# Summing the log forget gates of all blocks and heads with two matrix products, later in the index stage

## The chip, the cores and the metric

The kernel runs on one core of one Trainium2 chip. The metric is the device time of one execution in microseconds (us); the figure of a kernel is the median of its runs.

## The reference: what is computed

A trunk of two identical layers works on 1024 tokens behind 16 learned meta tokens. Each layer has one input projection, four groups of attention heads A, B, C and D, an output projection and a layer norm. The change touches one ingredient of group A (forgetting attention) alone: the running sum of the log forget gates, which is added to the logits as a decay.

```python
logf = jax.nn.log_sigmoid(h['a_f'].astype(jnp.float32) + b_f.astype(jnp.float32))
decay = jnp.transpose(jnp.cumsum(logf, axis=1), (0, 2, 1))
out_a = causal_dense_attention(qa, ka, va, key_valid, HEAD_DIM ** -0.5, decay)
# in it, for each block of 128 queries:
logits = logits + cq[..., None] - decay[:, :, None, :]
```

The part of a query, `cq`, is the same for all its keys and falls out of the softmax, so the kernel adds only the part of the keys. Group C picks 256 keys for every query by a score, a sum over 8 index heads of relu(q k) times a weight; the stage that computes this score is called the index stage here, and it is where the running sum is made.

## The kernel before, in words

Tokens stand in 9 blocks: block 0 has the 16 meta tokens, blocks 1 to 8 have 128 each. A class `Plan` writes one list of items by hand, and each engine walks through this list in order, doing its own part of every item and waiting on semaphores for the others. So the order of the list is the order of work on every engine; nothing reorders it.

The index stage (`Plan.index`) runs over four pairs of index heads, p = 0 to 3, and in each over the query blocks i = 8 down to 2. An item `ix` is: TensorE multiplies the block's queries with the keys in chunks of up to 512 columns into PSUM banks 0 to 3 (L993), two chunks in flight (`next_slot` alternates between banks 0, 1 and banks 2, 3); ScalarE applies the relu into one of three rows in SBUF (L1181); VectorE multiplies with the head's weight and accumulates the score (L1372, L1375). Between them stand fill items, taken from the list `fills[p]`, one after each `ix` while they last: a projection tile of a weight ring (L967) or a block of values of group A (`token_block`, L934). They use bank 4 (`P_BANK`), and ScalarE empties it. For p = 0 there are five fills, after i = 8 to 4, so that none stands after i = 3 or i = 2; for p = 1 and 2 it is the same.

The item `cum` stands after `ix` of p = 0, i = 3. VectorE computes log sigmoid of 9 blocks x 8 heads = 72 values for each of 128 token positions (L1340 to L1356, each instruction linked to the one ahead by a semaphore), with one exponential on ScalarE in between (L1135). TensorE then forms the running sums: for each group of three blocks, `c`, one bank of 8 rows (heads) x 384 columns (tokens), and for each block `b` up to it a product of the block's 128 x 8 gates with ones or with the upper triangle (L957), 18 products in all. ScalarE copies banks 0, 1 and 2 out with three instructions (L1138 to L1140). SyncE stores the 8 x 1040 result to DRAM (`falls`, L815) and, once it is stored, loads it back spread over 128 partitions (`load_fall`, L746), two rows for each pair of heads of group A. GpSimd adds the causal triangle to it (L1521), and the softmax of group A reads it (VectorE, L1449).

The semaphores around it: TensorE waits for `cum_in` (VectorE's last gate instruction) and for the banks to be free; ScalarE waits for `fe_in` ahead of the exponential and for `cum_full` ahead of the copies; the next `ix` on TensorE waits for `cum_free`, the last of these copies; SyncE's store waits for `cum_free` too.

Of the kernel before, what the change touches and what calls it, by code (L numbers as in the profile page):

```python
# [7 lines left out]
ALU = mybir.AluOpType  # L8
ACT = mybir.ActivationFunctionType

D_MODEL, SEQ, DEPTH = 1024, 1024, 2
N_META, BLK = 16, 128
NB = SEQ // BLK + 1
NTOK = SEQ + N_META
KT = D_MODEL // BLK
HD, NH = 64, 8
# [19 lines left out]
P_BANK = 4  # L36
# [15 lines left out]
def tok0(b):  # L52
    return 0 if b == 0 else N_META + BLK * (b - 1)


def rows_of(b):
    return N_META if b == 0 else BLK
# [81 lines left out]
class Plan:  # L139
# [156 lines left out]
    def index(self, l):  # L296
        fills = [[], [], [], []]
        for p in range(3):
            fills[p] += self.tile(l, "IQ", p=p + 1)
            fills[p] += [lambda b=b: self.token_block(l, "TA", b) for b in range(3 * p, 3 * p + 3)]  # L300
        fills[3] = self.tile(l, "AQ", p=0) + self.tile(l, "AK", p=0)
        for p in range(NP):
            for i in range(NB - 1, 1, -1):
                row = {8: 0, 7: 1, 6: 2, 5: 0, 4: 1, 3: 2, 2: 1}[i]
                n = keys_of(i)
                chunks = []
                for c0, w in even(n, -(-n // 512)):
                    ix = self.take("ix")
                    bank = self.next_slot()
                    chunks.append(dict(c0=c0, w=w, bank=bank, ix=ix,  # L310
                                       waits=self.banks([bank, bank + 1], ("relu_done", 2 * (ix + 1)))))
                acc = self.take("acc", 2)
                rwaits = latest([self.row_owner[row]] if self.row_owner[row] else [])
                self.row_owner[row] = ("acc_done", acc + 2)
                self.add("ix", l=l, p=p, i=i, n=n, chunks=chunks, acc=acc, row=row, rwaits=rwaits)
                if p == 0 and i == 3:
                    cum = self.take("cum")
                    self.add("cum", l=l, cum=cum, waits=self.banks([0, 1, 2], ("cum_free", cum + 1)))
                if fills[p]:
                    fills[p].pop(0)()  # L320

# [150 lines left out]
def build(nc, t_in, out):  # L472
# [4 lines left out]
    falls = [nc.dram_tensor(f"falls{l}", (NH, NTOK), F32, kind="Internal") for l in range(DEPTH)]  # L477
# [5 lines left out]
    with ctx:  # L483
# [55 lines left out]
        cT = sb("cT", [BLK, 3, NTOK])  # L539
        cT_flat = cT[:, :, :].rearrange("p a t -> p (a t)")  # L540
        w_out += [cT_flat[:, k * D_MODEL:(k + 1) * D_MODEL] for k in range(3)] + w_out_late
        falls_sb = cT[0:NH, 2, :]
        fall = [[cT[:, 0], cT[:, 1]], [feat[:, 4], feat[:, 5]]]
        gate = sb("gate", [BLK, NTOK])
        mixg = sb("mixg", [BLK, 2, 256])
# [2 lines left out]
        ident = sb("ident", [BLK, BLK])  # L548
        causal = sb("causal", [BLK, NTOK], BF16)
        tri_b = causal[:, NTOK - BLK:NTOK]  # L550
        upper1 = mixg[:, 0:2, :].rearrange("p g q -> p (g q)")
        rel = sb("rel", [32, 2 * NH])
        onehot = cT[0:32, 1, 0:2 * LINE]
        lmask = cT[0:NH, 0, 0:2 * LINE]
# [2 lines left out]
        rowmask = small[:, 0:1]  # L557
# [18 lines left out]
        fw = cT[:, 0, 0:6 * 72].rearrange("p (a b) -> p a b", a=6)  # L576
        f3 = [fw[:, j, :].rearrange("p (b h) -> p b h", b=NB) for j in range(6)]
# [4 lines left out]
        ps_s = ctx.enter_context(nc.psum_tensor("ps_s", [BLK, 5, 512], F32))  # L582
# [8 lines left out]
        S = {n: sem(n) for n in names}  # L591
# [117 lines left out]
        def _(sp):  # L709
# [80 lines left out]
            for it in items:  # L790
                kind, l = it["kind"], it["l"]
                if kind == "ln":
                    ln = it["ln"]
                    for n in ([] if it["first"] else [ln - 1]) + ([ln] if it["last"] else []):
                        sp.wait_ge(S["ln_done"], n + 1)
                        c = plan.ln_block[n]
# [15 lines left out]
                    sp.dma_start(turned[l].ap(), kr_own).then_inc(S["turn_st"], 16)  # L812
                elif kind == "cum":
                    sp.wait_ge(S["cum_free"], it["cum"] + 1)
                    sp.dma_start(falls[l].ap(), falls_sb).then_inc(S["fall_st"], 16)  # L815
                    sp.wait_ge(S["fall_st"], 16 * (l + 1))
                    load_fall(l, 0)
                elif kind == "mt":
                    if it["last"] and (it["wt"] % MT_PER_LAYER) < MT_PER_LAYER - 2:
# [6 lines left out]
                elif kind == "qk" and it["part"] == 0 and it["idx"] == 0:  # L826
                    br, p = it["br"], it["p"]
# [11 lines left out]
                    if br == "D" and p == 1:  # L839
                        sp.wait_ge(S["max_done"], end_of[(l, "A", NP - 1)])  # L840
                        src = bass.AP(turned[l], 0, [[0, BLK // ROPE], [NTOK, ROPE], [1, NTOK]])
# [29 lines left out]
                elif kind == "yl":  # L871
                    yy, b, ln = it["yy"], it["b"], it["ln"]
# [15 lines left out]
        def _(pe):  # L888
            pe.wait_ge(S["id_ld"], 16)
            for it in items:  # L890
                kind, l = it["kind"], it["l"]
                if kind == "pro":
# [3 lines left out]
                    for j in range(2):  # L896
                        mm = pe.matmul(ps_s[0:NH, 1 + j, 0:LINE], rel[:, NH * j:NH * (j + 1)],
                                       onehot[:, LINE * j:LINE * (j + 1)], start=True, stop=True)
                    mm.then_inc(S["line_full"], 1)
                elif kind == "xt":  # L900
                    M = rows_of(it["b"])
                    pe.wait_ge(S["ln_done"], it["ln"] + 1)
                    for j in range(2):
                        tg = it["tg"] + j
                        bank_left(pe, tg)
                        for c in range(4):
                            k = 4 * j + c
                            mm = pe.transpose(ps_t[:, tg % 2, c * BLK:c * BLK + M],
                                              x_new[0:M, it["ln"] % 2, k * BLK:(k + 1) * BLK], ident[0:M, 0:M])
                        mm.then_inc(S["t_full"], 1)  # L910
                elif kind == "tm":
                    b, what, bank = it["b"], it["what"], it["bank"]
# [35 lines left out]
                elif kind == "cum":  # L948
# [1 line left out]
                    if l > 0:  # L950
                        pe.wait_ge(S["up_ld"], 16 * l)
                    waits(pe, it["waits"])
                    for c in range(3):
                        for b in range(3 * c + 3):
                            j = max(b - 3 * c, 0)
                            src = upper1[:, 0:(3 - j) * BLK] if b >= 3 * c else upper1[:, BLK:4 * BLK]
                            mm = pe.matmul(ps_s[0:NH, c, j * BLK:3 * BLK], f3[5][:, b, :], src,  # L957
                                           start=(b == 0), stop=True, skip_group_check=(b > 0))
                    mm.then_inc(S["cum_full"], 1)
                elif kind == "mt":  # L960
                    wt, bank, (c0, w) = it["wt"], it["bank"], it["cols"]
# [108 lines left out]
        def _(act):  # L1070
# [9 lines left out]
            for it in items:  # L1080
# [43 lines left out]
                elif kind == "ct":  # L1124
# [5 lines left out]
                        a = nc.scalar.activation(cT[:, j, tok0(b):tok0(b) + M], ps_t[:, tg % 2, j * BLK:j * BLK + M],  # L1130
                                                 ACT.Copy, scale=gain)
                    a.then_inc(S["t_act"], 1)
                elif kind == "cum":
                    act.wait_ge(S["fe_in"], it["cum"] + 1)
                    nc.scalar.activation(fw[:, 2, :], fw[:, 1, :], ACT.Exp, scale=-1.0).then_inc(S["fe_out"], 1)  # L1135
                    act.wait_ge(S["cum_full"], it["cum"] + 1)
                    act.wait_ge(S["line_stored"], 32)
                    nc.scalar.activation(falls_sb[:, 0:N_META], ps_s[0:NH, 0, 0:N_META], ACT.Copy, scale=-1.0)  # L1138
                    nc.scalar.activation(falls_sb[:, N_META:272], ps_s[0:NH, 0, BLK:3 * BLK], ACT.Copy, scale=-1.0)
                    nc.scalar.activation(falls_sb[:, 272:NTOK].rearrange("p (c t) -> p c t", c=2),  # L1140
                                         ps_s[0:NH, 1:3, 0:3 * BLK], ACT.Copy, scale=-1.0).then_inc(S["cum_free"], 1)
                elif kind == "mt":
                    what, bank, (c0, w) = it["what"], it["bank"], it["cols"]
                    act.wait_ge(S["pj_full"], it["g"] + 1)
# [66 lines left out]
        def _(dve):  # L1211
            chain = [0]

            def link(ins):
                chain[0] += 1
                ins.then_inc(S["dve_chain"], 1)
                dve.wait_ge(S["dve_chain"], chain[0])
# [44 lines left out]
            for it in items:  # L1262
# [71 lines left out]
                elif kind == "iw":  # L1334
# [1 line left out]
                    dve.wait_ge(S["pj_dve"], it["upto"]["pj_dve"])  # L1336
                    dve.tensor_scalar(iws, fz[:, :, NH:2 * NH], IW_SCALE, None, ALU.mult).then_inc(S["iws_done"], 1)
                    dve.wait_ge(S["iws_done"], l + 1)
                elif kind == "cum":
                    link(dve.tensor_tensor(f3[0], fz[:, :, 0:NH], bf[:, 72 * l:72 * (l + 1)]  # L1340
                                           .rearrange("p (b h) -> p b h", b=NB), ALU.add))
                    link(dve.tensor_scalar(fw[:, 1, :], fw[:, 0, :], -1.0, None, ALU.mult))
# [10 lines left out]
                    link(dve.scalar_tensor_tensor(acc, acc, 1.0, s_, ALU.add, ALU.mult))  # L1353
                    link(dve.tensor_scalar(fw[:, 0, :], fw[:, 0, :], 0.0, None, ALU.min))
                    link(dve.scalar_tensor_tensor(fw[:, 5, :], acc, -2.0, fw[:, 0, :], ALU.mult, ALU.add))
                    dve.tensor_scalar(f3[5][:, 0, :], f3[5][:, 0, :], rowmask, None, ALU.mult).then_inc(S["cum_in"], 1)  # L1356
                elif kind == "ix":
                    i, n, acc = it["i"], it["n"], it["acc"]
                    sc = score[:, s_off[i]:s_off[i] + n]
# [289 lines left out]
```

## Time and profile before

| | |
|---|---|
| median of 3 runs | 3240.5 us (3233.13 to 3242.5) |
| the profiled execution | 3242.47 us, its span 3240.7 us |
| TensorE busy | 3023.3 us, 93% of the span |
| VectorE, ScalarE, GpSimd busy | 52%, 32%, 18% |
| mean granted TensorE clock | 0.983 of full speed |
| instructions L957 (running sums) | 72 records, 36 in each layer, first at 154.1 us, last at 1761.8 us |
| TensorE idle ahead of L957, for VectorE | 30.6 us |

The profile's span runs from the first to the last instruction. In the table of slices each digit is a tenth of a 81 us slice. A single-precision product leaves two records of matmul in the trace for each matmul of the program, so 18 products are 36 records. In a timeline row, square brackets hold the idle time of the engine just ahead of the row and what ended it; "issue" there is time in which the engine waited for nothing that the profile shows.

### The profile page before, as it was taken

Reading aid. Unit: us, or ns where it says so; the run is one execution under the profiler, and the core shown is the slowest. Engines: PE = TensorE matmul, PEld = TensorE weight load, DVE = VectorE, ACT = ScalarE, POOL = GpSimd, SP = SyncE. Lnnn points to the kernel's source line nnn. Section 1 sums busy time; section 2 is a strip of 40 time slices with the busy share of each in tenths; the row PEclk is TensorE's granted clock in tenths of the full one; section 3 lists DMA queues with packets and bytes.
Section 4 is the critical chain, followed back from the end, with each engine's and each line's share of the span. In section 5 each row is a group of like instructions: output and inputs, shape, how many; then the busy total and the mean of one; then the engine's idle time right before and its main releaser. Section 6 shows DMA issues by size and latency. Waiting matters only on the chain. (4 is left out here: it accounts for less than half of the span.)

```text
span 3240.7 us, 39947 instructions
## 1 busy us (share of the span) xinstructions
PE 3023.3 (93%) x14214; PEld 1734.7 (54%) x14214; DVE 1690.1 (52%) x4523; ACT 1021.1 (32%) x2749; POOL 568.7 (18%) x994
## 2 busy tenths in 40 slices
PE   6899999989899999989998999998998999999999
PEld 4445666555455555544453456665554556555443
DVE  4225887766677434421132378777667764444122
ACT  1223333333444433310012233333444443333000
POOL 1000222121112133310000012221111211333000
PEclk8999999999999999999999999999999999999999
DMA  5101110101000012042121011101010000200321
GB/s 204 48 27 33 40 40 30 40 30 48 16 21 16 22 32 93 14 154 78 52 69 30 12 35 47 42 30 38 29 51 14 16 16 30 90 30 24 125 73 52
DMA packets 91004, 153.05 MB, mean 47 GB/s; under 512 B 12656, under 2 KB 68224, under 8 KB 88504
## 3 DMA queue, kind: packets, MB, share of 16 engines
q1 hardware_dynamic: 90808, 150.50, 14.0%
q8 instruction: 115, 1.88, 0.2%
q14 instruction: 81, 0.66, 0.1%
HBM read 120.36 MB, written 32.21 MB: 47 GB/s over the span
## 5 line engine op out<-in xcount | busy, mean ns | idle before, releaser
L967 PE MATMUL ps_s<-xT,w_ring 128*128 128x348 f32 (+2 forms) x3616 | 1131.3, 467 | 4.3 <-DVE gate L1386 2.6
L967 PEld LDWEIGHTS ps_s<-xT,w_ring 128*128 128x128 f32 x3616 | 672.6, 191 | 395.2 <-issue 97.8
L1548 POOL TENSOR_SCALAR arena<-arena,small 128x256 f32<-128x256 f32 (+9 forms) x576 | 363.3, 642 | 1559.5 <-DVE small L1461 1558.3
L1196 ACT ACTIVATE arena<-arena,small 128x256 f32<-128x256 f32 (+9 forms) x576 | 380.3, 660 | 160.2 <-DVE small L1449 159.9
L1207 ACT ACTIVATE arena<-ps_t 128x512 f32<-128x512 f32 (+4 forms) x700 | 309.2, 472 | 363.1 <-PE ps_t L1034 353.7
L1034 PE MATMUL ps_t<-ident,arena 128*128 128x128 f32 (+2 forms) x2432 | 355.9, 274 | 49.2 <-ACT arena L1207 33.7
L1237 DVE MAX8 small<-score 128x8 f32<-128x1040 f32 (+6 forms) x448 | 376.4, 840 | 10.5
L1239 DVE MATCH_REPLACE8 score<-small,score 128x1040 f32<-128x1040 f32 (+6 forms) x448 | 370.0, 826 | 0.0
L1034 PEld LDWEIGHTS ps_t<-ident,arena 128*128 128x128 f32 (+2 forms) x2432 | 252.7, 131 | 207.6 <-issue 97.9
L1011 PE MATMUL ps_s<-feat 64*128 64x256 f32 (+12 forms) x1888 | 306.9, 426 | 28.8 <-DVE small L1449 24.1
L1046 PE MATMUL ps_o<-arena 128*64 128x256 f32 (+3 forms) x2816 | 311.1, 357 | 20.7 <-ACT cT L1130 12.3
L1061 PE MATMUL ps_s<-arena,feat 128*128 128x512 f32 x640 | 287.2, 602 | 10.4 <-DMA arena<-in_w_out 10.4
L1046 PEld LDWEIGHTS ps_o<-arena 128*64 128x64 f32 (+1 forms) x2816 | 179.0, 136 | 151.9 <-issue 55.3
L1011 PEld LDWEIGHTS ps_s<-feat 64*128 64x128 f32 (+1 forms) x1888 | 145.8, 179 | 139.8 <-issue 67.8
L1286 DVE SCALAR_TENSOR_TENSOR arena<-score,ps_s 128x512 f32<-128x512 f32 (+1 forms) x34 | 23.4, 687 | 377.5 <-PE ps_s L1061 357.2
L1061 PEld LDWEIGHTS ps_s<-arena,feat 128*128 128x128 f32 x640 | 123.1, 193 | 163.8 <-issue 151.3
L934 PE MATMUL ps_s<-arena,xT 128*128 128x272 f32 (+1 forms) x512 | 183.4, 514 | 11.1 <-ACT xT L1091 5.0
L1375 DVE SCALAR_TENSOR_TENSOR score<-arena,small,score 128x1040 f32<-128x1040 f32 (+6 forms) x98 | 88.0, 901 | 175.6 <-ACT arena L1181 169.7
L934 PEld LDWEIGHTS ps_s<-arena,xT 128*128 128x128 f32 x512 | 99.0, 199 | 85.3 <-issue 74.6
L1164 ACT ACTIVATE gate<-ps_s 128x348 f32<-128x348 f32 (+1 forms) x96 | 44.2, 460 | 307.3 <-PE ps_s L967 307.3
L1413 DVE COPY arena<-ps_t 128x384 f32<-128x384 f32 (+4 forms) x124 | 65.2, 528 | 142.5 <-PE ps_t L1034 142.1
L1449 DVE CUSTOM_DVE_ANT_0 arena<-ps_s,causal 128x512 f32<-128x512 f32 (+5 forms) x144 | 57.9, 437 | 152.9 <-PE ps_s L1022 152.0
(147 smaller groups left out, 2342.2 us busy)
## 6 DMA issues: line engine op xcount, KB each, us to landing
w_ring<-in_w_feat SPq DMA_DIRECT2D x78, 512.0 KB, 3.5
mixed<-mixg SPq DMA_DIRECT2D x128, 128.0 KB, 1.7
feat<-mixed SPq DMA_DIRECT2D x16, 1024.0 KB, 6.6
resid<-score SPq DMA_DIRECT2D x16, 512.0 KB, 3.1
score<-resid SPq DMA_DIRECT2D x16, 512.0 KB, 7.4
arena<-in_w_out SPq DMA_DIRECT2D x4, 1536.0 KB, 8.1
cT<-falls SPq DMA_DIRECT2D x8, 520.0 KB, 5.0
feat<-falls SPq DMA_DIRECT2D x8, 520.0 KB, 5.3
```

What stands on the lines that cost most here:

```text
L934: mm = pe.matmul(ps_s[0:M, bank, 0:n], xT[:, k, cols], wv[:, k, :], start=(k == 0), stop=(k == KT - 1))
L967: mm = pe.matmul(ps_s[:, bank, 0:w], w_ring[:, wt % 2, k, :], xT[:, k, c0:c0 + w], start=(k == 0), stop=(k == KT - 1))
L1011: mm = pe.matmul(ps_s[0:M, ch["bank"] + e, 0:ch["w"]], q[r:r + HD, qc], k[r:r + HD, k0 + ch["c0"]:k0 + ch["c0"] + ch["w"]], start=True, st ...
L1034: mm = pe.transpose(ps_t[0:w, tg % 2, c * BLK:c * BLK + M], p_row(it, h, k0, w), ident[0:M, 0:M])
L1046: mm = pe.matmul(ps_o[HD * e:HD * e + HD, at:at + w], v_of(br, p, e, kb), arena[0:rows_of(kb), src:src + w], start=(j == 0), stop=(j == le ...
L1061: mm = pe.matmul(ps_s[0:M, bank, :], mix_in[slot][:, k, 0:M], w_out[k][:, cols], start=(k == 0), stop=(k == 15))
L1196: nc.scalar.activation(p, p, ACT.Exp, scale=-1.0, bias=nm[:, e:e + 1], accum_out=psums[0:M, st % 4, e:e + 1]).then_inc(S["exp_done"], 1)
L1207: a = nc.scalar.activation(dst, src, ACT.Copy)
L1237: dve.max(top8, sc).then_inc(S["top_step"], 1)
L1239: dve.match_replace(sc, top8, sc, TAKEN).then_inc(S["top_step"], 1)
L1375: dve.scalar_tensor_tensor(sc, src, w, sc, ALU.mult, ALU.add).then_inc(S["acc_done"], 1)
L1548: nc.gpsimd.tensor_scalar(p, p, rinv[0:M, st % 4, e:e + 1], 1.0, ALU.mult, ALU.mult).then_inc(S["nrm_done"], 1)
```

## The change

The running sum is split in two parts. VectorE first adds up, for each head and each token position, the gates of all earlier blocks: slot 3 of `fw` is cleared for block 0 (a memset) and then filled by 8 linked additions of 128 x 8, block by block. Two products with all 72 columns (block, head) as stationary operand then give everything at once: the gates with the triangle (the sum inside the block), and the sums over earlier blocks with a 128 x 128 square of ones. The result is 72 rows x 128 columns in bank 4. ScalarE copies it with one instruction, and SyncE stores it with nine DMAs of 8 rows, one for each block.

The item is also split. The gate computation of VectorE and ScalarE keeps its place (item `lf`, after p = 0, i = 3); the products, the copy and the DMAs (item `cum`) stand after p = 1, i = 6, ahead of the fill that follows there. The item now waits for bank 4 in place of banks 0, 1 and 2.

```diff
                 if p == 0 and i == 3:
+                    self.add("lf", l=l, cum=self.n["cum"])
+                if p == 1 and i == 6:
                     cum = self.take("cum")
-                    self.add("cum", l=l, cum=cum, waits=self.banks([0, 1, 2], ("cum_free", cum + 1)))
+                    self.add("cum", l=l, cum=cum, waits=self.banks([P_BANK], ("cum_free", cum + 1)))
...
-        falls_sb = cT[0:NH, 2, :]
+        falls_sb = cT[0:NB * NH, 2, 0:BLK]
...
-                    sp.dma_start(falls[l].ap(), falls_sb).then_inc(S["fall_st"], 16)
-                    sp.wait_ge(S["fall_st"], 16 * (l + 1))
+                    for b in range(NB):
+                        sp.dma_start(falls[l].ap()[:, tok0(b):tok0(b) + rows_of(b)],
+                                     falls_sb[NH * b:NH * (b + 1), 0:rows_of(b)]).then_inc(S["fall_st"], 16)
+                    sp.wait_ge(S["fall_st"], 16 * NB * (l + 1))
                     load_fall(l, 0)
...
-                    for c in range(3):
-                        for b in range(3 * c + 3):
-                            j = max(b - 3 * c, 0)
-                            src = upper1[:, 0:(3 - j) * BLK] if b >= 3 * c else upper1[:, BLK:4 * BLK]
-                            mm = pe.matmul(ps_s[0:NH, c, j * BLK:3 * BLK], f3[5][:, b, :], src,
-                                           start=(b == 0), stop=True, skip_group_check=(b > 0))
+                    for k, src in ((5, upper1[:, 0:BLK]), (3, upper1[:, BLK:2 * BLK])):
+                        mm = pe.matmul(ps_s[0:NB * NH, P_BANK, 0:BLK], fw[:, k, :], src, start=(k == 5), stop=(k == 3))
                     mm.then_inc(S["cum_full"], 1)
...
-                    nc.scalar.activation(falls_sb[:, 0:N_META], ps_s[0:NH, 0, 0:N_META], ACT.Copy, scale=-1.0)
-                    nc.scalar.activation(falls_sb[:, N_META:272], ps_s[0:NH, 0, BLK:3 * BLK], ACT.Copy, scale=-1.0)
-                    nc.scalar.activation(falls_sb[:, 272:NTOK].rearrange("p (c t) -> p c t", c=2),
-                                         ps_s[0:NH, 1:3, 0:3 * BLK], ACT.Copy, scale=-1.0).then_inc(S["cum_free"], 1)
+                    nc.scalar.activation(falls_sb, ps_s[0:NB * NH, P_BANK, 0:BLK], ACT.Copy, scale=-1.0
+                                         ).then_inc(S["cum_free"], 1)
...
-                    dve.tensor_scalar(f3[5][:, 0, :], f3[5][:, 0, :], rowmask, None, ALU.mult).then_inc(S["cum_in"], 1)
+                    dve.memset(f3[3][:, 0, :], 0.0)
+                    link(dve.tensor_scalar(f3[5][:, 0, :], f3[5][:, 0, :], rowmask, None, ALU.mult))
+                    for b in range(1, NB):
+                        t = dve.tensor_tensor(f3[3][:, b, :], f3[3][:, b - 1, :], f3[5][:, b - 1, :], ALU.add)
+                        if b < NB - 1:
+                            link(t)
+                    t.then_inc(S["cum_in"], 1)
```

TensorE in layer 0, the end of p = 0 and the start of p = 1, before: `ps_s<-feat` are the products of the score (400 columns is i = 3, 272 is i = 2, 348 and 344 are i = 8 of p = 1), `mixg,cT` the running sums.

```order
L993 MATMUL ps_s<-feat 128x400 x2
L957 MATMUL ps_s<-mixg,cT 8x384
L957 MATMUL ps_s<-mixg,cT 8x256
L957 MATMUL ps_s<-mixg,cT 8x128
L957 MATMUL ps_s<-mixg,cT 8x384 x4
L957 MATMUL ps_s<-mixg,cT 8x256
L957 MATMUL ps_s<-mixg,cT 8x128
L957 MATMUL ps_s<-mixg,cT 8x384 x7
L957 MATMUL ps_s<-mixg,cT 8x256
L957 MATMUL ps_s<-mixg,cT 8x128
L993 MATMUL ps_s<-feat 128x272 x2
L993 MATMUL ps_s<-feat 128x348 x4
```

TensorE from the same place on, after the change (the score's products are now L994, the ring tile L968, the values L938):

```order
L994 MATMUL ps_s<-feat 128x400 x2
L994 MATMUL ps_s<-feat 128x272 x2
L994 MATMUL ps_s<-feat 128x348 x4
L994 MATMUL ps_s<-feat 128x344 x2
L968 MATMUL ps_s<-xT,w_ring 128x448 x8
L994 MATMUL ps_s<-feat 128x456 x4
L968 MATMUL ps_s<-xT,w_ring 128x448 x8
L994 MATMUL ps_s<-feat 128x392 x4
L959 MATMUL ps_s<-mixg,cT 72x128 x2
L938 MATMUL ps_s<-arena,xT 128x512 x8
```

The 18 products between i = 3 and i = 2 are gone, and two stand between i = 6 of p = 1 and the values of a block that follow it.

VectorE at the end of the gate computation, before:

```order
L1355 SCALAR_TENSOR_TENSOR cT<-cT 128x72
L1356 TENSOR_SCALAR cT<-cT,small 128x8
L1372 TENSOR_SCALAR score<-arena,small 128x272
L1375 SCALAR_TENSOR_TENSOR score<-arena,small,score 128x272
L1375 SCALAR_TENSOR_TENSOR score<-arena,small,score 128x1040 x2
```

And after the change:

```order
L1355 SCALAR_TENSOR_TENSOR cT<-cT 128x72
L1356 MEMSET cT 128x8
L1357 TENSOR_SCALAR cT<-cT,small 128x8
L1359 TENSOR_TENSOR cT<-cT 128x8 x8
L1378 TENSOR_SCALAR score<-arena,small 128x272
L1381 SCALAR_TENSOR_TENSOR score<-arena,small,score 128x272
L1381 SCALAR_TENSOR_TENSOR score<-arena,small,score 128x1040 x2
```

Nine small instructions stand ahead of the score of i = 2.

## Rows read from the trace of the kernel before

**Rows 1.** The page: busy time by engine, and tenths by slice.

```profile
PE 3023.3 (93%) x14214; PEld 1734.7 (54%) x14214; DVE 1690.1 (52%) x4523; ACT 1021.1 (32%) x2749; POOL 568.7 (18%) x994
...
PE   6899999989899999989998999998998999999999
...
PEclk8999999999999999999999999999999999999999
```

**Rows 2.** Timeline, layer 0, around the sums (start, length, engine, line, count, idle).

```profile
145.81 0.94 PE L993 MATMUL ps_s<-feat 64*128 64x400 f32 x4
...
146.85 0.90 ACT L1181 ACTIVATE arena<-ps_s 128x400 f32<-128x400 f32 x2 [0.33 <-PE ps_s L993]
...
149.23 0.26 ACT L1135 ACTIVATE cT<-cT 128x72 f32<-128x72 f32 x1 [1.49 <-DVE cT L1343]
...
153.80 0.23 DVE L1356 TENSOR_SCALAR cT<-cT,small 128x8 f32<-128x8 f32 x1
...
154.09 12.69 PE L957 MATMUL ps_s<-mixg,cT 128*8 128x384 f32 x36 [7.33 <-DVE cT L1356]
...
166.90 0.36 ACT L1139 ACTIVATE cT<-ps_s 8x256 f32<-8x256 f32 x1
...
168.00 1.31 PE L993 MATMUL ps_s<-feat 64*128 64x272 f32 x8 [1.22 <-ACT cT L1140]
...
169.73 0.50 DVE L1375 SCALAR_TENSOR_TENSOR score<-arena,small,score 128x272 f32<-128x272 f32 x1
...
171.05 6.28 PE L967 MATMUL ps_s<-xT,w_ring 128*128 128x448 f32 x16
```

**Rows 3.** Timeline, layer 1, TensorE at the same place.

```profile
1742.28 0.94 PE L993 MATMUL ps_s<-feat 64*128 64x400 f32 x4
...
1750.55 11.48 PE L957 MATMUL ps_s<-mixg,cT 128*8 128x384 f32 x36 [7.33 <-DVE cT L1356]
...
1763.25 1.31 PE L993 MATMUL ps_s<-feat 64*128 64x272 f32 x8 [1.22 <-ACT cT L1140]
...
1766.30 5.91 PE L967 MATMUL ps_s<-xT,w_ring 128*128 128x448 f32 x15
```

**Rows 4.** Timeline, layer 0, the same sequence between p = 1 and p = 2.

```profile
210.30 1.40 PE L993 MATMUL ps_s<-feat 64*128 64x400 f32 x8
...
212.38 1.44 PE L993 MATMUL ps_s<-feat 64*128 64x348 f32 x8 [0.68 <-ACT arena L1181]
...
214.16 0.85 PE L993 MATMUL ps_s<-feat 64*128 64x344 f32 x4 [0.34 <-ACT arena L1181]
...
214.94 6.28 PE L967 MATMUL ps_s<-xT,w_ring 128*128 128x448 f32 x16
```

**Rows 5.** Timeline, layer 0, p = 1, i = 6 and the fill behind it.

```profile
185.20 1.59 PE L993 MATMUL ps_s<-feat 64*128 64x392 f32 x8
...
186.22 1.67 ACT L1181 ACTIVATE arena<-ps_s 128x392 f32<-128x392 f32 x4 [0.37 <-PE ps_s L993]
...
186.72 7.13 PE L934 MATMUL ps_s<-arena,xT 128*128 128x512 f32 x16
```

**Rows 6.** The page's costliest groups: matmuls with 128 columns.

```profile
L1034 PE MATMUL ps_t<-ident,arena 128*128 128x128 f32 (+2 forms) x2432 | 355.9, 274 | 49.2 <-ACT arena L1207 33.7
```

**Rows 7.** Timeline, layer 0, a tile of values behind a wait.

```profile
128.93 8.80 PE L934 MATMUL ps_s<-arena,xT 128*128 128x512 f32 x16 [2.20 <-DVE arena L1330]
```

**Rows 8.** Windows of TensorE alone: stretch, length, busy, granted clock, DMA.

```profile
129.00:130.00 1.00, 1.00 (x2) 0.57 0.00 0
...
1726.00:1728.00 2.00, 0.91 (x2) 1.00 0.00 0
```

**Rows 9.** Timeline, layer 0: load of the sums, its first readers.

```profile
169.75 0.81 SPq L746 DMA_DIRECT2D cT<-falls  x2
...
175.26 0.81 POOL L1521 TENSOR_TENSOR cT<-cT,causal 128x128 f32<-128x128 f32 x2 [109.88 <-DMA cT<-falls]
...
297.28 0.52 DVE L1449 CUSTOM_DVE_ANT_0 arena<-ps_s,cT 128x348 f32<-128x348 f32 x1
```

More of the change, by code:

```diff
@@ L550, in build @@
         tri_b = causal[:, NTOK - BLK:NTOK]
-        upper1 = mixg[:, 0:2, :].rearrange("p g q -> p (g q)")
+        upper1 = mixg[:, 0, :]
         rel = sb("rel", [32, 2 * NH])
@@ L1132, in _ @@
                     a.then_inc(S["t_act"], 1)
-                elif kind == "cum":
+                elif kind == "lf":
                     act.wait_ge(S["fe_in"], it["cum"] + 1)
                     nc.scalar.activation(fw[:, 2, :], fw[:, 1, :], ACT.Exp, scale=-1.0).then_inc(S["fe_out"], 1)
+                elif kind == "cum":
                     act.wait_ge(S["cum_full"], it["cum"] + 1)
                     act.wait_ge(S["line_stored"], 32)
-                    nc.scalar.activation(falls_sb[:, 0:N_META], ps_s[0:NH, 0, 0:N_META], ACT.Copy, scale=-1.0)
-                    nc.scalar.activation(falls_sb[:, N_META:272], ps_s[0:NH, 0, BLK:3 * BLK], ACT.Copy, scale=-1.0)
-                    nc.scalar.activation(falls_sb[:, 272:NTOK].rearrange("p (c t) -> p c t", c=2),
-                                         ps_s[0:NH, 1:3, 0:3 * BLK], ACT.Copy, scale=-1.0).then_inc(S["cum_free"], 1)
+                    nc.scalar.activation(falls_sb, ps_s[0:NB * NH, P_BANK, 0:BLK], ACT.Copy, scale=-1.0
+                                         ).then_inc(S["cum_free"], 1)
                 elif kind == "mt":
@@ L1338, in _ @@
                     dve.wait_ge(S["iws_done"], l + 1)
-                elif kind == "cum":
+                elif kind == "lf":
                     link(dve.tensor_tensor(f3[0], fz[:, :, 0:NH], bf[:, 72 * l:72 * (l + 1)]
@@ L1614 @@
     arrays["ident"] = np.eye(BLK, dtype=f32)
-    arrays["upper1"] = np.concatenate([np.triu(np.ones((BLK, BLK), f32)), np.ones((BLK, 3 * BLK), f32)], 1)
+    arrays["upper1"] = np.concatenate([np.triu(np.ones((BLK, BLK), f32)), np.ones((BLK, BLK), f32)], 1)
     small = np.zeros((BLK, 24), f32)
```

## The prediction, made before the changed kernel had run

> **What bounds the kernel now.** I read the page first. TensorE is busy 93% of the span, in 36 of 40 slices at least eight tenths of the time, and the granted clock is at nine tenths or more in all but one slice [rows 1]. VectorE, the next engine, is at 52%. So the time falls if TensorE has less to do or waits less, and other engines count where TensorE waits for them. Next I read the timeline around the running sums. There TensorE issues the two products of p = 0, i = 3 at 145.81, then stands idle for 7.33 us until VectorE has the last gate, works 12.69 us on the 36 records, and waits 1.22 us more for the last copy [rows 2]. Both layers show this, with 7.33, 11.48 and 1.22 us [rows 3]. In the two stretches nothing else runs on TensorE, and nothing behind it can go ahead, since each engine takes the items in order. That is 7.33 + 12.69 + 1.22 = 21.2 us and 7.33 + 11.48 + 1.22 = 20.0 us, on the path in full.
>
> **What goes.** The best measure of the place without the sums is in the trace itself: between p = 1 and p = 2 the same score products follow each other with no item between. From the first product of i = 3 to the ring tile behind i = 8 it takes 214.94 - 210.30 = 4.64 us [rows 4]. The same piece with the sums takes 171.05 - 145.81 = 25.24 us in layer 0 [rows 2] and 1766.30 - 1742.28 = 24.02 us in layer 1 [rows 3]. If the place ran like its twin, the gain would be 20.60 + 19.38 = 40.0 us.
>
> **What stays there.** It won't run quite like its twin, since `lf` keeps its place on VectorE and ScalarE. Count from the start of i = 3 on TensorE. ScalarE ends the relus of i = 3 at 146.85 + 0.90, that is at 1.94 us, then waits for VectorE, and ends the exponential at 149.23 + 0.26, at 3.68 us [rows 2]. Before, nothing was queued behind this exponential but the wait for the sums. Now the relus of i = 2 are, and behind them those of i = 8 of p = 1. Two relus of 400 columns take 0.90 us [rows 2]; I scale this to 0.7 us for the two of i = 2, which end at 4.4. TensorE has by then done i = 2 and the first chunk of i = 8, and has waited for these banks. Its second chunk runs from 4.45 to 5.2 (half of the 1.44 us for two chunks [rows 4]). The relus of the first chunk, another 0.8 us by the same scaling, end at 5.2, so the third chunk starts at 5.3 and the ring tile 0.78 us later (214.94 - 214.16 [rows 4]), at 6.1 us. The twin has 4.64, so the exponential costs 1.45 us in each layer. The gain of the place is 25.24 - 6.1 = 19.1 and 24.02 - 6.1 = 17.9, together 37.0 us. Bounds: no cost (40.0) if relus and products fit better than I think; at worst the new wait of about 1.7 us between the first and the second chunk lets the clock fall, which is priced under the rivals.
>
> **VectorE's additions.** They lengthen the gate computation by a memset and 8 linked additions on 128 x 8. The instruction nearest to them, the masking of block 0, is 128 x 8 and takes 0.23 us [rows 2], with its semaphore some 0.27; nine make 2.4 us, so the gates end at 154.03 + 2.4, 10.6 us after the start of i = 3. Behind them VectorE has the score of i = 2, about 1 us (two instructions of 272 columns, the second 0.50 us [rows 2]), done at 11.6. Who waits for that? ScalarE's relu of i = 7, p = 1, which needs the row of i = 2; its product comes behind the ring tile, at 6.1 + 6.28 = 12.4 us [rows 2]. The cover is the ring tile and the slack 0.8 us. If each addition took twice as long, VectorE would be 2.4 us later and ScalarE 1.6 us late, of which TensorE's next tile hides most, since TensorE waits only for banks. I take zero. The products themselves are asked for only at i = 6, more than 20 us after i = 3, so the wait for VectorE (7.33 us) is gone and not moved.
>
> **What comes in behind i = 6 of p = 1.** Two products with 128 columns, four records. The nearest row has 128 columns at 355.9 / 2432 = 0.146 us a record [rows 6], so 0.6 us of work, and about 0.8 until the result can be read. They start where the tile of values starts now, at 186.72. But the tile wants bank 4, and so waits for ScalarE's copy, and this stands behind the four relus of i = 6, which end at 186.22 + 1.67 = 187.89 [rows 5]. The copy of 72 x 128 lies near the one of 256 columns, 0.36 us [rows 2], and I take 0.26. With the semaphore the tile starts at 188.25, in place of 186.72: 1.5 us in each layer, 3.1 us in all. Lower bound 0.6 us (the records alone), upper bound 2.3 us (four records at 0.274 us one after the other, at half clock, then a copy of 0.36). The bank's own last tile has been emptied by then.
>
> **SyncE.** Nine stores for one. They start at about the same absolute time as before, since the item is 18 us later in the list and the list 18 us ahead. Between the load's issue and its landing lie 175.26 - 169.75 = 5.5 us, and the first softmax instruction of group A that reads it stands at 297.28 [rows 9]. I cost them at nothing: the rest of the index stage, over 100 us, is their cover. What is queued behind them on SyncE is the next tile of the weight ring, asked for two tiles ahead.
>
> **Sum.** 37.0 - 3.1 = 33.9 us less. Against the profiled execution's own 3242.47 us that gives 3208.6; this execution was 2.0 us above the median of the runs, 3240.5, so I forecast 3206.6 us. Of the gain about 24 us are work of TensorE (12.69 + 11.48) and the rest is waiting.
>
> **Rivals.**
>
> A. *The clock falls at the new waits.* In layer 0 a wait of 2.20 us stands ahead of a tile of values, the clock falls to 0.57 just behind it, which is the step from 2.4 to 1.2 GHz, and the tile takes 8.80 us [rows 7, 8], where the same tile takes 7.13 us at full clock [rows 5]: 1.7 us. At the like place of layer 1 the clock stayed at 1.00 [rows 8]. Now there would be a wait of 1.7 us in the score and one of 0.9 us behind the sums, in both layers: at most 4 x 1.7 = 6.7 us, a gain of 27, 3213 us. Against it: both new waits are shorter than the one that lowered the clock once in two. The Trainium skill has a rule for it ("TensorE: Matmul & The Clock Gate", section "A second HAM failure mode: psum-queue depth-cycling"): short idles between groups of matmuls that wait for PSUM can make the clock swing between half and full rate, and the price is paid between the bursts. By that rule all four waits would cost. In this trace short waits of 0.68 and 0.34 us recur at every i = 8 without it.
>
> B. *Everything fits as at the twin*, and the copy waits for nothing: 40.0 - 2 x 0.6 = 38.8 us less, 3202 us. Against it stands the order of ScalarE's queue.
>
> C. *Part is given back later.* A stage behind might be set by VectorE or a DMA that does not start sooner. TensorE is busy at nine tenths in nearly all slices of group A [rows 1], and nothing there waits for a fixed time, so I see no taker; if half were lost, 3223 us.
>
> D. *Slower: the sums reach group A too late.* The place is the first softmax of group A and GpSimd's addition ahead of it. It decides only when the nine stores and the load need longer than the rest of the index stage. Before, the load had landed 297.28 - 175.26 = 122 us ahead of its reader [rows 9]; some 18 us of that go with the shorter list, which leaves 104. Only behind that would TensorE stand, and the kernel would be slower once the delay is over 104 + 34 us: at 150 us more, 3252 us. Nine stores would have to take more than 15 us each; one store and the wait for it fit into the 1.75 us between TensorE's release at 168.00 and the load's issue at 169.75 [rows 2, 9]. The Trainium skill ("DMA: Bandwidth & Descriptors", section "Anatomy of one DMA — SWDGE (gpsimd) path") gives each DMA a fixed cost of about 2.0 us; nine of them one behind another would be 18 us, an estimate from that page, and hidden too.
>
> **Chances.** The forecast, with its own range of 3200 to 3213 us: 0.73. A: 0.13 (in full or in part). B: 0.08. C: 0.05. D: 0.01. The range takes in A and B, the bounds of the two terms (a gain of 26 to 39 us) and the spread of the runs, which reached 7 us below the median and 2 above: 3197 to 3217 us. A measurement of this kernel can't tell less than about 0.3%, 10 us, from no change. Forecast, A, B and most of C are beyond that: faster 0.97, no change 0.02, slower 0.01.
>
> **What the changed profile should show.** No wait of 7.33 us for VectorE ahead of the sums; from i = 3 of p = 0 to the ring tile about 6.1 us in both layers; two products of 72 x 128 behind i = 6 of p = 1, four records, and then an idle of about 0.9 us for ScalarE's copy ahead of the tile of values; nine stores and a load that lands more than 90 us ahead of group A. TensorE's busy time should fall by about 23 us. I am wrong if the stretch of i = 3 stays above 8 us, if the clock falls behind it, or if group A or a later stage takes longer than before.

## The result, and the profile after

The changed kernel takes 3202.8 us (median of 4 runs, 3199.75 to 3203.75) against 3241.5 us before (now the median of 4 runs, 3233.13 to 3242.85): a ratio of 0.9884, 95% interval 0.9866 to 0.9903. That is 38.7 us less; forecast were 33.9 us less and 3206.6 us. A second set of runs gave 3204.0 against 3239.4 us, 35.4 us less. The profiled execution took 3199.75 us, its span is 3198.0 us, 42.7 us less than the profiled one before.

The page of the changed kernel, the lines that answer to [rows 1]:

```profile
PE 2991.0 (94%) x14150; PEld 1724.7 (54%) x14150; DVE 1692.6 (53%) x4541; ACT 1019.1 (32%) x2745; POOL 572.8 (18%) x994
...
PE   6999999999899999989999999998988999998998
...
PEclk9999999999999999999999999999999999999999
```

TensorE has 64 records less (72 went, 8 came) and works 32.3 us less, and the one slice with a clock under nine tenths is gone. The change also halves the constant `upper1` to 256 columns, which the description of the change leaves out; ahead of the sums that shows in no steady way: at 125 us one of the three profiles of the changed kernel (two come from the experiments) is ahead of all four of before, and two are behind them all. The next fence is the timeline of layer 0 at the old place of the sums, from i = 3 of p = 0 to the ring tile (start, length, engine, line, shape, count, and in brackets the idle time ahead and its releaser); it answers to [rows 2].

```profile
143.20 1.40 PE L994 MATMUL ps_s<-feat 64*128 64x400 f32 x8
...
145.28 0.86 PE L994 MATMUL ps_s<-feat 64*128 64x348 f32 x4 [0.68 <-ACT arena L1181]
...
146.62 0.26 ACT L1136 ACTIVATE cT<-cT 128x72 f32<-128x72 f32 x1 [1.48 <-DVE cT L1343]
146.78 1.37 ACT L1181 ACTIVATE arena<-ps_s 128x272 f32<-128x272 f32 x4
...
147.50 2.68 PE L994 MATMUL ps_s<-feat 64*128 64x348 f32 x8 [1.37 <-ACT arena L1181]
...
150.11 6.62 PE L968 MATMUL ps_s<-xT,w_ring 128*128 128x448 f32 x16
...
151.45 1.57 DVE L1359 TENSOR_TENSOR cT<-cT 128x8 f32<-128x8 f32 x8
```

The wait of 7.33 us for VectorE and the 36 records are gone. (The 30.6 us for this wait in the table of before count it twice, once for TensorE's products and once for its weight loads; the products' own wait is 2 x 7.33 = 14.7 us.) In their place stands the wait of 1.37 us for the relus queued behind the exponential: at 146.62 ScalarE had been idle for 1.48 us with the products of i = 2 ready for it. VectorE's eight additions come later, beside the ring tile, and nobody waits for them. The piece took 150.11 - 143.20 = 6.91 us, and behind the wait the clock fell (two chunks in 2.68 us). In layer 1 it did not. This is TensorE there, at the old place and behind the sums at the new one, to be held against [rows 3]:

```profile
1724.08 1.40 PE L994 MATMUL ps_s<-feat 64*128 64x400 f32 x8
...
1728.38 1.55 PE L994 MATMUL ps_s<-feat 64*128 64x348 f32 x8 [1.37 <-ACT arena L1181]
...
1729.87 6.28 PE L968 MATMUL ps_s<-xT,w_ring 128*128 128x448 f32 x16
...
1746.99 7.10 PE L938 MATMUL ps_s<-arena,xT 128*128 128x512 f32 x16 [0.80 <-ACT cT L1140]
```

Here it is 1729.87 - 1724.08 = 5.79 us. Of the new place behind i = 6 of p = 1 the timeline of layer 0 shows, beside [rows 5] and [rows 9]:

```profile
166.12 0.66 PE L959 MATMUL ps_s<-mixg,cT 128*72 128x128 f32 x4
...
167.15 0.28 ACT L1140 ACTIVATE cT<-ps_s 72x128 f32<-72x128 f32 x1
167.46 2.99 SPq L818 DMA_DIRECT2D falls<-cT  x9
167.58 7.10 PE L938 MATMUL ps_s<-arena,xT 128*128 128x512 f32 x16 [0.80 <-ACT cT L1140]
171.38 0.82 SPq L748 DMA_DIRECT2D cT<-falls  x2
...
176.94 1.93 POOL L1527 TENSOR_TENSOR cT<-cT,causal 128x128 f32<-128x128 f32 x2 [111.98 <-DMA cT<-falls]
...
278.11 0.52 DVE L1455 CUSTOM_DVE_ANT_0 arena<-ps_s,cT 128x348 f32<-128x348 f32 x1
```

The tile of values starts 1.46 us after the sums' first product, 0.80 us of it idle for ScalarE's copy. The load has landed by 176.94, 101 us ahead of its reader.

So the place of the change gives 25.24 - 6.91 = 18.33 and 24.02 - 5.79 = 18.23 us, less 0.34 us by which the ring tile of layer 0 is slower (6.62 against 6.28 us), less 1.46 and 1.45 us at the new place: 33.3 us. The spans differ by 42.7. The 9.4 us between the two are what the experiments had to find first.

### The profile page after: what moved, and what is told of

The parts are those of the page before. It is cut to its first block and busy times, and to the rows that moved or that the text cites. A ratio compares the mean times of both kernels' runs of the same rounds, so it can differ in the third digit from the quotient of the medians.

```text
span 3198.0 us, 39847 instructions
## 1 busy us (share of the span) xinstructions
PE 2991.0 (94%) x14150; PEld 1724.7 (54%) x14150; DVE 1692.6 (53%) x4541; ACT 1019.1 (32%) x2745; POOL 572.8 (18%) x994
## 5 line engine op out<-in xcount | busy, mean ns | idle before, releaser
L968 PE MATMUL ps_s<-xT,w_ring 128*128 128x348 f32 (+2 forms) x3616 | 1130.5, 466 | 4.3 <-DVE gate L1392 2.6
L968 PEld LDWEIGHTS ps_s<-xT,w_ring 128*128 128x128 f32 x3616 | 672.2, 191 | 394.8 <-issue 97.0
L1035 PE MATMUL ps_t<-ident,arena 128*128 128x128 f32 (+2 forms) x2432 | 356.0, 274 | 49.4 <-ACT arena L1207 33.9
L938 PE MATMUL ps_s<-arena,xT 128*128 128x272 f32 (+1 forms) x512 | 180.7, 507 | 12.7 <-ACT xT L1092 5.0
L938 PEld LDWEIGHTS ps_s<-arena,xT 128*128 128x128 f32 x512 | 97.8, 196 | 84.8 <-issue 74.4
```

The source lines that it names most:

```text
L938: mm = pe.matmul(ps_s[0:M, bank, 0:n], xT[:, k, cols], wv[:, k, :], start=(k == 0), stop=(k == KT - 1))
L968: mm = pe.matmul(ps_s[:, bank, 0:w], w_ring[:, wt % 2, k, :], xT[:, k, c0:c0 + w], start=(k == 0), stop=(k == KT - 1))
L1035: mm = pe.transpose(ps_t[0:w, tg % 2, c * BLK:c * BLK + M], p_row(it, h, k0, w), ident[0:M, 0:M])
```

## The experiments

**Where the other 9 us are: both kernels once more, unchanged.** If the stages behind the index stage had become faster through the change, the same lead would be there in any pair of profiles. Two theories stood against each other: falls of TensorE's clock that one execution has and another hasn't, or an effect of the change.

> The changed kernel once more, unchanged. Theory (what the profiles show beyond 33 us at the place of the change is the clock of TensorE falling in other stages in one execution and not in another): its profile has its drops at other places than the first one, so that leads over the kernel before of 1 to 2 us come and go in the stages of layer 1, and the timed gain is 33 to 40 us. Rival (a later stage really became faster): the same stages of layer 1 show the same 7 us again, drop for drop.

> The kernel before once more, unchanged, one look. Theory (5 to 9 us of what the first pair of profiles shows beyond the place of the change are falls of the clock that one execution has and another hasn't): outside the sums its time at half clock differs from the first profile's 96 us by several us, and stages that this change doesn't touch start up to some us earlier or later. Rival (the kernel before always has the additional falls in layer 1): its falls stand at the same places and sum to the same 96 us.

> The kernel before, one more look. Outside the sums its two profiles had 96 and 82 us at half clock at 3242.5 and 3234.3 us. Theory (each fall of the clock costs half its length, wherever it comes): the time follows 3193 us + 0.5 x (us at half clock outside the sums) within 2 us. Rival (the runs near 3240 us are longer for another reason): a run near 3240 us with only 82 us at half clock.

> The same again, to see how often the kernel before has the additional falls in the stages behind the index stage of layer 1. Theory and rival as in the third look; most of the timed runs of the kernel before lie at 3239 to 3243 us, so I expect one of the two looks there, with 90 us or more at half clock outside the sums.

> The changed kernel, a third look. Outside the place of the change its two profiles had 76 and 82 us at half clock at 3199.8 and 3204.8 us. Theory: again 76 to 87 us, and the time is near 3161 us + 0.5 x that, within 2 us. Rival (the change moved later stages against each other): falls of the clock at places where the kernel before never has one.

Measured, with the time at half clock (1.2 GHz) added up from the granted clock, inside the span and apart from the falls at the old place of the sums (the expectations count 2 us more for the first profiles, the part of the last fall that lies behind the span):

| profile | time, us | at half clock elsewhere, us |
|---|---|---|
| before, first | 3242.5 | 94 |
| before, second | 3234.3 | 80 |
| before, third | 3241.6 | 94 |
| before, fourth | 3233.6 | 73 |
| after, first | 3199.8 | 74 |
| after, second | 3204.8 | 80 |
| after, third | 3202.2 | 73 |

The unchanged kernel before differs by up to 8.8 us between its own profiles. Three falls that the first and third have and the others lack can be looked up. Windows of TensorE alone (stretch, length, busy and count, granted clock, DMA) in the first profile of before:

```profile
1894.00:1897.00 3.00, 3.00 (x8) 0.50 0.63 230
2536.00:2538.00 2.00, 2.00 (x4) 0.50 0.04 8
2604.00:2607.00 3.00, 3.00 (x7) 0.50 0.00 0
```

The same windows in its second profile:

```profile
1894.00:1897.00 3.00, 3.00 (x11) 1.00 0.05 19
2536.00:2538.00 2.00, 2.00 (x13) 1.00 0.00 0
2604.00:2607.00 3.00, 3.00 (x25) 1.00 0.00 0
```

In the third they are at 0.62, 0.50 and 0.63, in the fourth at 1.00. The kernel is the same and TensorE is fully busy in all of them, and in 2604 to 2607 it starts 7 records in place of 25. By the clock the profiles have drifted apart by some us, so a window doesn't hold quite the same products; the traces settle this when the 14142 products outside the sums are matched one by one. Between the first and the fourth profile of before, the lead of the fourth grows by 1.65 us at 1894 to 1898, by 1.7 us at 2534 to 2540 and by 1.7 us at 2603 to 2610. Between the first profiles of before and after, the lead of the changed kernel is 0.9 us at 60 us, and from there on, outside the two places, it moves in steps of 1.0 to 1.7 us, up and down (down at 936 to 944, at 1068 to 1076 and at 2468), nearly each beside a fall that stands in the one profile and not in the other; all that is left beside these steps is 0.3 us. So the rival falls: no stage that the change left alone became faster, and none gave anything back (rival C of the prediction). The first pair had 20 us less at half clock elsewhere, and half of that, 10 us, is near the 9.4 us left over. The average over the four profiles of before is 3238.0 us and over the three of after 3202.3 us, 35.7 us less. My rule of half a microsecond for each at half clock fails its own bound of 2 us: with the figures of the table it missed the fourth profile of before by 4.0 us (3229.6 expected, 3233.6 measured) and the third of after by 4.7 us, and counted as the expectations count, by 3.0 and 3.6 us. One reason can be read: at 1412 to 1415 us of its trace the second profile of before has 3.4 us at half clock that the fourth hasn't, while TensorE stands idle for a DMA (5.00 us there, 5.25 in the fourth), and against the fourth the products behind come no later, within 0.1 us. What decides which falls an execution gets stays open.

**The two parts one at a time.** First only the place: 18 products as before, moved behind i = 6 of p = 1.

```diff
                 if p == 0 and i == 3:
+                    self.add("lf", l=l, cum=self.n["cum"])
+                if p == 1 and i == 6:
                     cum = self.take("cum")
...
```

> The 18 products are kept, but they stand behind i = 6 of p = 1, and the gates stay behind i = 3 of p = 0. Theory (place and product count add up): the stretch from i = 3 to the ring tile falls to 5.8 to 6.9 us as after the change (-18 us a layer); behind i = 6 there come about 1.2 us of wait for banks 0 to 2 and 36 records at full clock, 24 x 0.32 + 6 x 0.22 + 6 x 0.11 = 9.7 us, 10.9 us a layer. Together 36 - 22 = 14 us faster than before, about 3227 us. Rival (the gain is nearly all from the stall; the products were cheap): over 25 us faster, under 3216 us.

Measured: 3222.7 us, ratio to before 0.9946 (0.9931 to 0.9961), 16.6 us less, where about 14 were expected. Timeline of TensorE, layer 0, at the new place:

```profile
166.22 1.59 PE L995 MATMUL ps_s<-feat 64*128 64x392 f32 x8
...
169.05 9.85 PE L959 MATMUL ps_s<-mixg,cT 128*8 128x384 f32 x36 [1.24 <-ACT arena L1184]
...
178.83 7.13 PE L936 MATMUL ps_s<-arena,xT 128*128 128x512 f32 x16
```

The wait for three banks is 1.24 us and the products take 9.85 us at full clock, where they took 12.69 at the old place, the first 5.7 us of it at the lowered clock [rows 2]. 178.83 - 166.22 = 12.6 us against 1.5 without the sums is a cost of 11.1 us; expected were 10.9. Since the tile behind them uses another bank, it doesn't wait for the copies.

Then only the products: two of them and the additions, at the old place.

```diff
                 if p == 0 and i == 3:
                     self.add("lf", l=l, cum=self.n["cum"])
-                if p == 1 and i == 6:
                     cum = self.take("cum")
```

> The two products and the 8 additions, at the old place behind i = 3 of p = 0. Theory: TensorE stands idle until the additions end, 9.85 us after the start of i = 3 (8.9 us idle, in place of 7.33), then 0.7 to 0.9 us of products; the ring tile starts at about 13.8 us and loses some 2 us to a lowered clock. Against 25.2 and 24.0 us before that is 11.4 + 10.2 - 2 = about 20 us faster, near 3222 us; with e1 it adds up to the whole gain. Rival (the place is what counts): under 10 us faster, over 3231 us.

Measured: 3217.7 us, ratio 0.9931 (0.9915 to 0.9948), 21.7 us less. Timeline of TensorE, layer 0:

```profile
153.00 1.13 PE L958 MATMUL ps_s<-mixg,cT 128*72 128x128 f32 x4 [8.94 <-DVE cT L1358]
...
154.06 4.24 PE L993 MATMUL ps_s<-feat 64*128 64x272 f32 x16
...
158.23 6.28 PE L967 MATMUL ps_s<-xT,w_ring 128*128 128x448 f32 x16
```

The wait grew to 8.94 us, since the additions stand ahead of the products, and nearly all that follows up to the ring tile runs at the lowered clock: 158.23 - 143.12 = 15.1 us for the piece, where I had 13.8 and the loss in the ring tile. Both rivals fall. The parts add up but for some 1 to 3 us: 16.6 + 21.7 = 38.3 us, and the whole change was 35.4 us against the same runs of before; at the places alone the traces of both layers give 15.5 + 19.1 = 34.6 us against 33.3. Each removes what the other can't: the place removes the wait, the form removes the work.

**VectorE's additions, three times over.**

```diff
-                    for b in range(1, NB):
+                    for b in [b for _ in range(3) for b in range(1, NB)]:
...
```

> After the change, with the 8 additions of VectorE made three times over (the same values again). Theory (the ring tile and the slack behind it cover VectorE): 16 more additions of 0.19 us are 3.1 us a layer on VectorE, the row of i = 2 comes free 3.1 us later, some 13.5 us after the start of i = 3, where ScalarE asks for it at about 14; TensorE waits for nothing more, same time as the changed kernel within 1 us. Rival (VectorE's time there shows): 2 x 3.1 = 6 us slower.

Measured: 3203.8 us (3202.87 to 3204.23), as the changed kernel (3202.8 and 3204.0). In the timeline, layer 0, VectorE's additions and TensorE's next score product:

```profile
152.18 4.78 DVE L1362 TENSOR_TENSOR cT<-cT 128x8 f32<-128x8 f32 x24
...
157.38 1.80 PE L994 MATMUL ps_s<-feat 64*128 64x456 f32 x8
```

The additions take 4.78 in place of 1.57 us, and the product of i = 7 comes 157.38 - 143.93 = 13.45 us after the start of i = 3, within a hundredth of where it comes without them (156.66 - 143.20 = 13.46). That the additions cost nothing is shown.

**The sums in the last place.** The item `cum` behind p = 3, i = 2, so that the stores and the load stand bare.

```diff
-                if p == 1 and i == 6:
+                if p == NP - 1 and i == 2:
```

> After the change, with the products, the copy and the DMAs put behind the last score product of the index stage (p = 3, i = 2), so that no work covers the stores and the load. Theory (the 100 us between the load and group A are what hides nine stores): copy, nine issues of 0.33 us, about 0.9 us of wait and 5.5 us of load bring the first softmax of group A some 9 us later, 7.5 to 10 us a layer net: 15 to 20 us slower than the changed kernel, about 3220 us. Rival (each of the nine stores costs about 2 us, one behind another): over 35 us slower.

Measured: 3224.1 us, ratio to before 0.9957 (0.9942 to 0.9972), some 20 to 21 us slower than the changed kernel, at the upper end of the 15 to 20 that I expected. The timeline of layer 0:

```profile
275.81 3.00 SPq L818 DMA_DIRECT2D falls<-cT  x9
...
279.75 0.82 SPq L748 DMA_DIRECT2D cT<-falls  x2
...
286.05 0.52 DVE L1455 CUSTOM_DVE_ANT_0 arena<-ps_s,cT 128x348 f32<-128x348 f32 x1 [9.19 <-DMA cT<-falls]
...
287.07 1.52 PE L1012 MATMUL ps_s<-feat 64*128 64x344 f32 x4 [10.24 <-DVE small L1455]
```

The same product of TensorE in the changed kernel, and the one store of the kernel before:

```profile
279.14 0.85 PE L1012 MATMUL ps_s<-feat 64*128 64x344 f32 x4 [1.38 <-DVE small L1455]
```

```profile
167.97 0.27 SPq L815 DMA_DIRECT2D falls<-cT  x1
```

The nine stores are issued in 3.00 us and all done 0.94 us later: 3.94 us, against 1.78 for the one store before (167.97 to the load's issue at 169.75 [rows 9]). So the time of one store isn't paid nine times over; that would be 16 us. TensorE waits 10.24 us where it waited 1.38, which is 8.9 us more in this layer (9.1 in the other), and behind the wait the lowered clock stretches the same product and the ring tile that follows it from 5.7 to 7.6 us. Against this some 1.4 us a layer are saved behind i = 6. The rival (over 35 us) falls, and the mechanism of my rival D is shown to exist: in the changed kernel it is covered by some 100 us of other work.

**Without the two new waits.** The gates behind p = 1, i = 8, where no relu is queued behind the exponential, and the products in the PSUM bank of the output products (`ps_o`), which the tile of values doesn't use.

```diff
-                if p == 0 and i == 3:
+                if p == 1 and i == 8:
                     self.add("lf", l=l, cum=self.n["cum"])
...
-                        mm = pe.matmul(ps_s[0:NB * NH, P_BANK, 0:BLK], fw[:, k, :], src, start=(k == 5), stop=(k == 3))
+                        mm = pe.matmul(ps_o[0:NB * NH, 0:BLK], fw[:, k, :], src, start=(k == 5), stop=(k == 3))
...
```

> As after the change, but the gates are computed behind i = 8 of p = 1 (so no relu stands behind the exponential's wait), and the two products write the PSUM bank of the output products, which is idle in the index stage, so the tile of values needn't wait for the copy. Theory: i = 3 to the ring tile takes 4.64 us as at the twin (now 5.8 and 6.9), the tile of values starts 0.66 us after the score's products in place of 1.46, without idle time; 1.2 + 2.3 + 2 x 0.8 = about 4 to 5 us faster than the changed kernel, about 3198 us. Rival (VectorE or ScalarE then wait at i = 7 of p = 1, which needs the row of i = 2): TensorE waits some 2 us there and the kernel is no faster than after the change.

Measured: 3197.3 us (3196.12 to 3200.31), ratio to before 0.9869 (0.9854 to 0.9884); the changed kernel beside it took 3204.0 (3199.5 to 3204.82). So it is the fastest by the medians, by 6.7 us; the two ranges overlap by 0.8 us, and no interval between these two was taken. The timeline of TensorE, layer 0:

```profile
143.36 1.40 PE L994 MATMUL ps_s<-feat 64*128 64x400 f32 x8
...
145.44 1.44 PE L994 MATMUL ps_s<-feat 64*128 64x348 f32 x8 [0.68 <-ACT arena L1181]
...
148.00 6.28 PE L968 MATMUL ps_s<-xT,w_ring 128*128 128x448 f32 x16
...
163.67 0.66 PE L959 MATMUL ps_o<-mixg,cT 128*72 128x128 f32 x4
164.16 7.03 PE L938 MATMUL ps_s<-arena,xT 128*128 128x512 f32 x16
```

148.00 - 143.36 = 4.64 us is the twin of [rows 4] to the hundredth, and the tile of values starts 0.49 us after the sums. In the traces this is worth 2.61 us (with the ring tile) + 1.15 us at the old place and 2 x 0.97 us at the new one, 5.7 us; I had written 4 to 5. Its profiled execution, 3200.31 us, is even so no shorter than the first of the changed kernel (3199.75 us): it had 85 us at half clock elsewhere, against 74. So the gain is read from the place, and the total of one profile would have hidden it. The rival, a wait at i = 7, didn't come.

## Why the prediction was right

*The bound.* TensorE's queue set the time at this place, and what left it left the span: shown by the two parts, 16.6 and 21.7 us.

*The old place.* Predicted 6.1 us from i = 3 to the ring tile in both layers and a gain of 37.0 us; measured 6.91 and 5.79 us and 36.6 us, or 36.2 with the slower ring tile. The twin between p = 1 and p = 2 was the right scale, and the wait for the exponential was the right correction: without it the experiment runs at 4.64 us. That the sum came out so close is in part luck: at full clock the exponential costs 1.15 us a layer, where I had 1.45, and one fall of the clock, which the sum had at nothing, took 1.5 us.

*VectorE.* Predicted at nothing, behind a cover of the ring tile; shown by the tripled additions. Their size was overrated: 1.57 us for eight, where I had 0.27 us each.

*The new place.* Predicted 1.5 us a layer, set by ScalarE's relus ahead of the copy; measured 1.46 and 1.45. The idle time was 0.80 us where I had 0.9. My upper bound of 2.3 us doesn't follow from its terms: 4 x 0.274 + 0.36 is 1.5 us, and 0.274 us is the mean length of such a record over the whole page, not one at half clock. Nothing hung on it.

*SyncE.* Predicted at nothing, with 104 us of cover; there were 101. Stripped of the cover the same DMAs cost some 10 us a layer. The estimate of 18 us for nine stores one behind another (rival D) is not what they took: it was 3.94 us until all were done.

*The sum.* 33.9 predicted and 33.3 measured at the place. The timed gains of 38.7 and 35.4 us are larger because the median of before holds more of the executions with additional falls of the clock; the averages of the profiles give 35.7. How many falls a profile or a median catches is chance, so the 3.8 us between 3206.6 and 3202.8 us say nothing on the mechanism. They also put the time at rival B's figure, 3202 us, though B's mechanism didn't happen: the copy and the exponential were waited for, and the place gave 33.3 us and not 38.8. The experiment without the two new waits is B made real, and it gives 33.3 + 5.7 = 39.0 us there.

*Rival A* is partly true, and I gave it 0.13 in full or in part; by my own sign of being wrong, a clock that falls behind i = 3, the forecast failed on this point in one layer of every profile. In each of the three profiles of the changed kernel the clock fell at the new wait of one layer and not of the other (layer 0 in the first, layer 1 in the second and third); in the one with only the place changed it fell in neither, with the additions tripled in one, with the sums in the last place in both: 6 of 12 waits of 1.37 us in all. Without that wait, in the last experiment, it fell in neither layer. One fall costs 6.91 - 5.79 + 0.34 = 1.5 us. None of the waits of 0.80 us behind the sums lowered it. The section of the Trainium skill that I had named ("TensorE: Matmul & The Clock Gate", "A second HAM failure mode: psum-queue depth-cycling") tells of a kernel in which frequent short idles of this kind make the clock swing. This case shows such falls too, but that all four waits would pay, 6.7 us by my row, was my reading of it, and in each profile it was one of four.

*What failed.* TensorE's busy time fell by 32.3 us, not 23: busy time is longer at the lower clock, so that number mixes work and clock (the falls elsewhere are in it), and I shouldn't have used it as a test. And I misread the page in one place: TensorE is at eight tenths or more in 39 of the 40 slices, not 36, which only makes the case for it as the bound stronger.

## What to carry to other kernels

When a step is taken out of a queue that sets the time, look for the same sequence elsewhere in the trace without that step: it gives the new length better than a sum of durations, and then only what stays behind (here an exponential with relus queued behind it) has to be added. An item that waits for another engine belongs where that engine is already ahead, and its result into a bank that the next instruction doesn't need. Profile a kernel more than once before a difference under about 10 us in a stage that was not changed is given a cause.

## What was not expected of the hardware

The four profiles of one and the same kernel fall into two groups by where TensorE's clock fell, 7 to 9 us apart: 3242.5 and 3241.6 against 3234.3 and 3233.6 us. The first and third agree fall for fall, at places about 1 us apart. Whether there are only two is not shown: timed runs of this kernel at 3237.9 to 3239.5 us lie between them and have no profile. Nine DMAs of 4 KB or less from one queue took 0.33 us each to issue, and 0.94 us behind the last issue all were done; from its start, the one store of 32.5 KB took 1.78 us.
